# Norms at four seams of a two-layer diffusion trunk, split into token halves and placed beside weight products

## What is computed

```python
def rms_norm(x, g):
    y = xf * lax.rsqrt(jnp.mean(xf * xf, axis=-1, keepdims=True) + EPS)
    return (y * g.astype(jnp.float32)).astype(x.dtype)
def modulate(x, shift, scale):
    return x * (1 + scale) + shift
def ffn_sublayer(t, shift, scale, gate, g_pre, g_post, w_in, w_out):
    y = swiglu(modulate(rms_norm(t, g_pre), shift, scale), w_in, w_out)
    return t + FFN_RES * gate * rms_norm(y, g_post)
...
for l in range(DEPTH):
    x = ffn_sublayer(x, ...)            # sub 0, both streams
    px = project(modulate(rms_norm(x, g[2]), mx[3], mx[4]), mix_w_in[l])
    ya, yb, yc = mix_latent(...)        # three attentions
    y = merge_branches(ya, yb, yc, ...)
    x = x + mx[5] * rms_norm(y, g[3])   # sub 1
    x = ffn_sublayer(x, ...)            # sub 2
```

## Time and profile before

| | |
|---|---|
| median of 3 runs | 2990.26 us (2989.13 to 2990.41) |
| the profiled execution | 2989.05 us, its span 2987.3 us |
| PE busy | 2807.8 us, 94% |
| DVE busy | 1611.3 us, 54% |
| ACT busy | 1195.4 us, 40% |
| POOL busy | 230.9 us, 8% |
| DMA | 343.70 MB, mean 115 GB/s |

### The profile page before, as it was taken

The page is one execution under the profiler, slowest core; times in us unless marked ns, Lnnn a source line. Parts: engine busy times, 40 slices in busy tenths (PEclk is TensorE's granted clock), DMA queues, the critical chain, the costliest instruction groups (busy, mean ns, idle before and its releaser), DMA issues.

```text
span 2987.3 us, 40226 instructions
## 1 busy us (share of the span) xinstructions
PE 2807.8 (94%) x14410; PEld 2239.9 (75%) x14410; DVE 1611.3 (54%) x2722; ACT 1195.4 (40%) x2175; POOL 230.9 (8%) x321
## 2 busy tenths in 40 slices
PE   6999988999889999997999979999889989999998
PEld 4888866886656676785888848888679766869897
DVE  4677336636645444345576246773365465545764
ACT  3222324226545435434222242222343455555543
POOL 0001001101200000010000000000011020001000
PEclk8999998999999999998999989999989999999999
DMA  5455324321111122132454325553233211324554
GB/s 228 169 197 194 93 79 152 109 98 36 43 36 36 50 74 71 43 120 93 145 176 165 90 72 174 195 195 93 79 106 127 78 57 64 113 82 156 204 174 136
DMA packets 94956, 343.70 MB, mean 115 GB/s; under 512 B 10993, under 2 KB 12785, under 8 KB 92657
## 3 DMA queue, kind: packets, MB, share of 16 engines
q1 hardware_dynamic: 74850, 263.45, 26.2%
q0 software_dynamic: 19984, 78.65, 7.4%
HBM read 337.85 MB, written 4.20 MB: 115 GB/s over the span
## 4 chain that ended last, share of the span: by engine, by line
PE 78%; issue 9%; DVE 5%; ACT 5%; POOL 1%; DMA 1%; SPq 0%; POOLq 0%; DVEq 0%; ACTq 0%
PE ps L1726 20%; PE ps L1718 20%; PE ps L1719 20%; PE ps L823 3%; PE ps L785 3%; PE ps L802 2%; PE ps L1796 2%; PE ps L1778 1%; PE ps L1775 1%; PE ps L1780 1%; ACT work L1220 1%; PE ps L775 1%; DVE mx L673 1%; POOL acc L933 1%; ACT prob L589 1%
## 5 line engine op out<-in xcount | busy, mean ns | idle before, releaser
L1328 DVE TENSOR_TENSOR wlo<-raw,whi 128x1024 fp32r<-128x1024 f32 x492 | 597.8, 1224 | 689.0 <-ACT whi L1070 688.8
L1718 PE MATMUL ps<-xhi,whi 128*128 128x512 f32 (+1 forms) x2304 | 823.2, 368 | 53.2 <-DVE xlo L1562 44.8
L1719 PE MATMUL ps<-xlo,whi 128*128 128x512 f32 (+1 forms) x2304 | 811.3, 363 | 0.0
L1070 ACT ACTIVATE whi<-raw 128x1024 fp32r<-128x1024 f32 x492 | 520.6, 1058 | 564.4 <-PE ps L1726 493.9
L1718 PEld LDWEIGHTS ps<-xhi,whi 128*128 128x128 f32 x2304 | 443.8, 193 | 143.5 <-issue 44.4
L1726 PE MATMUL ps<-xhi,wlo 128*128 128x512 f32 (+1 forms) x2304 | 507.1, 363 | 0.0
L1719 PEld LDWEIGHTS ps<-xlo,whi 128*128 128x128 f32 x2304 | 445.4, 193 | 61.6
L1726 PEld LDWEIGHTS ps<-xhi,wlo 128*128 128x128 f32 x2304 | 396.1, 192 | 63.8 <-issue 0.7
L1476 DVE SCALAR_TENSOR_TENSOR work<-ada,work 128x1024 f32<-128x1024 f32 x256 | 299.5, 1221 | 0.2 <-DMA ada<-in_ada_rows 0.2
L1718 PE MATMUL ps<-ghi,whi 128*128 128x512 f32 (+1 forms) x704 | 252.2, 368 | 1.9 <-ACT whi L1070 1.9
L1719 PE MATMUL ps<-glo,whi 128*128 128x512 f32 (+1 forms) x704 | 251.8, 366 | 0.0
(11 more groups left out here) (201 smaller groups left out, 3329.1 us busy)
## 6 DMA issues: line engine op xcount, KB each, us to landing
raw<-in_ffn_in SPq DMA_DIRECT2D x176, 512.0 KB, 4.7
ada<-in_ada_rows POOLq DMA_DIRECT2D x128, 512.0 KB, 3.8
raw<-in_merge SPq DMA_DIRECT2D x96, 512.0 KB, 3.5
raw<-in_ffn_out SPq DMA_DIRECT2D x64, 512.0 KB, 3.5
raw<-in_qk_a SPq DMA_DIRECT2D x32, 512.0 KB, 3.5
raw<-in_ffn_out SPq DMA_DIRECT2D x32, 384.0 KB, 3.1
raw<-in_qk_b SPq DMA_DIRECT2D x20, 512.0 KB, 3.5
raw<-in_v_a SPq DMA_DIRECT2D x16, 512.0 KB, 3.5
```

Source lines behind the costliest of these rows:

```text
L1070: act.activation(whi[:, g.ring(SPLIT), :], raw[:, g.ring(RAW), :], ACT.Copy).then_inc(hi_ready, 1)
L1328: dve.tensor_tensor(wlo[:, g.ring(SPLIT), :], raw[:, g.ring(RAW), :], whi[:, g.ring(SPLIT), :].bitcast(F32), ALU.subtract).then_inc(lo_rea ...
L1718: pe.matmul(o, w, hi[:, first + c, 0:tk], start=start, stop=False)
L1719: pe.matmul(o, w, lo[:, first + c, 0:tk], start=False, stop=False)
```

## The change

1. The norms of the four 512-token seams are worked as two halves of 256 tokens (`half_norm`). The last products before the seam are run twice: the last 4 output tiles of `ffn_out` (12 groups), or all 8 groups of `wo`, first for tokens 0 to 255, then, with the weights loaded and split again, for tokens 256 to 511. The norm of the first half is interleaved with the second of these runs, one slot of the norm to a group (`beside`).
2. The norm of the second half is interleaved with the first products after the seam, done for the first half alone: in front of a feed-forward the first 8 groups of `ffn_in` (`head`, in eight PSUM banks), which are then run again for the second half; in front of the mixer the 10 groups of `v_b` and `v_a`, run for the first half and then for the second. The values thus come first in the mixer, ahead of the rope products. The remaining `ffn_in` has 9 bodies in place of 11 where a head was taken off (sub 2 of layer 0, sub 0 of layer 1).
3. POOL sums the squares of `x` over chunks (7 adds), and PE does one sum with ones in place of eight.
4. In all norms DVE now multiplies `x` by the scale and the inverse root in one instruction, and the shift goes in with ACT's rounding to `xhi` and with DVE's subtraction to `xlo`: ACT has one pass for a chunk in place of two. At 512 tokens each is two instructions of 256.

```diff
-TOKEN_BANKS = {"v_b": [4, 5, 6, 7], "v_a": [2, 3, 4, 5, 6, 7, 4, 5], "uv": [2, 3, 4, 5, 6, 7, 4, 5]}
+TOKEN_BANKS = {("v_b", 0): [2, 3], ("v_a", 0): [4, 5, 2, 3], ("v_b", 1): [4, 5], ("v_a", 1): [2, 3, 4, 5],
+               ("uv", 0): [2, 3, 4, 5, 6, 7, 4, 5]}
 STAT, ADA_BANK = 6, 7
+HALF_STAT = 7
+HEAD = 8
...
+def beside(norm, products):
+    for _ in products:
+        next(norm, None)
+    for _ in norm:
+        pass
...
+    def half_norm(layer, post, pre, half):
+        adds = {"stat": 2, "inv": 2, "gated": KC, "x": KC, "xsq": KC, "xsum": KC - 1, "scaled": KC, "xhi": KC,
+                "xlo": KC}
+        return add("norm", layer, post=post, pre=pre, tokens=S, span=(half * S, half * S + S), adds=adds, half=True)
+    def last_products(layer, post, pre, **kw):
+        add("y", layer, span=(0, S), fresh=not kw.get("first", 0), **kw)
+        first_half = half_norm(layer, post, pre, 0)
+        first_half.products = (add("y", layer, span=(S, T), **kw),)
...
-        def ffn(sub, tokens):
+        def ffn(sub, tokens, post, pre, head=None):
             made = vectors[(layer, sub)]
-            add("ffn_in", layer, sub=sub, tokens=tokens, iters=FC // 2, groups=4, tiles=4, vectors=made,
-                adds={"ghi": FC, "glo": FC, "made": sum(m % 3 > 0 for _, m in made)})
-            add("y", layer, src="ffn_out", sub=sub, tokens=tokens, iters=KC // 4, groups=12, tiles=4,
-                per_tile=3, adds={"sq": KC, "acc": KC})
-        ffn(0, T)
-        norm(layer, (layer, 0), (layer, 1), T)
+            first = 0
+            if head:
+                products = add("head", layer, src="ffn_in", sub=sub, tokens=S, iters=1, groups=HEAD, tiles=HEAD,
+                               head=True)
+                half_norm(layer, *head, 1).products = (products,)
+                add("ffn_in", layer, sub=sub, tokens=T, span=(S, T), iters=HEAD // 4, groups=4, tiles=4, head=True,
+                    adds={"ghi": HEAD // 2, "glo": HEAD // 2})
+                first = HEAD
+            add("ffn_in", layer, sub=sub, tokens=tokens, first=first, iters=(2 * FC - first) // 4, groups=4, tiles=4,
+                vectors=made,
+                adds={"ghi": FC - first // 2, "glo": FC - first // 2, "made": sum(m % 3 > 0 for _, m in made)})
+            kw = dict(src="ffn_out", sub=sub, tokens=tokens, groups=12, tiles=4, per_tile=3)
+            if tokens == S:
+                add("y", layer, iters=KC // 4, adds={"sq": KC, "acc": KC}, fresh=True, **kw)
+                norm(layer, post, pre, tokens)
+                return
+            kw.update(iters=1, adds={"sq": KC // 2, "acc": KC // 2})
+            add("y", layer, fresh=True, **kw)
+            last_products(layer, post, pre, first=KC // 2, **kw)
+        ffn(0, T, (layer, 0), (layer, 1), ((layer - 1, 2), (layer, 0)) if layer else None)
...
+        for half in range(2):
+            products = (
+                add("v", layer, src="v_b", cols=256, x="x", kpg=4, iters=1, groups=2, first=half, adds={"vk": 2}),
+                add("v", layer, src="v_a", cols=512, x="x", kpg=2, iters=2, groups=4, first=half, adds={"vk": 4}))
+            if half == 0:
+                half_norm(layer, (layer, 0), (layer, 1), 1).products = products
         blocks = list(range(KC)) if layer == 0 else []
+        add("rope", layer, src="qk_b", dst="q_b", first=0, tokens=nq, iters=2, groups=4, tiles=4, scale=HEAD_SCALE,
+            side=blocks[:KC // 2], adds={"rope": 8})
+        add("rope", layer, src="qk_b", dst="k_b", first=8, tokens=T, iters=1, groups=2, tiles=2, adds={"rope": 2})
...
-        add("y", layer, src="wo", sub=1, tokens=nq, iters=2, groups=4, tiles=4, per_tile=1,
-            adds={"sq": KC, "acc": KC})
-        norm(layer, (layer, 1), (layer, 2), nq)
-        ffn(2, nq)
-        norm(layer, (layer, 2), None if last else (layer + 1, 0), nq)
+        kw = dict(src="wo", sub=1, tokens=nq, iters=2, groups=4, tiles=4, adds={"sq": KC, "acc": KC})
+        if last:
+            add("y", layer, fresh=True, **kw)
+            norm(layer, (layer, 1), (layer, 2), nq)
+            ffn(2, nq, (layer, 2), None)
+        else:
+            last_products(layer, (layer, 1), (layer, 2), **kw)
+            ffn(2, nq, (layer, 2), (layer + 1, 0), ((layer, 1), (layer, 2)))
...
+            def normed_high(ph, c):
+                l, sub = ph.pre
+                act.wait_ge(done["scaled"], base(ph, "scaled") + c + 1)
+                for s in streams(ph.span):
+                    last = act.activation(xhi[:, c, sl(s)], work[:, c, sl(s)], ACT.Identity,
+                                          bias=mods[:, l, 3 * sub, c, s:s + 1])
+                last.then_inc(done["xhi"], 1)
+            def act_norm(ph):
+                inverse(HALF_STAT, ph.span, D, base(ph, "stat") + 1)
+                yield
+                yield
+                for chunks in ((0, 1, 2), (3, 4, 5), (6, 7)):
+                    for c in chunks:
+                        square(ph, c)
+                    yield
+                inverse(HALF_STAT, ph.span, D, base(ph, "stat") + 2)
+                yield
+                for chunks in ((0, 1), (2, 3, 4), (5, 6, 7)):
+                    for c in chunks:
+                        normed_high(ph, c)
+                    yield
...
+            def scaled(ph, c):
+                l, sub = ph.pre
+                for s in streams(ph.span):
+                    last = dve.scalar_tensor_tensor(work[:, c, sl(s)], x[:, c, sl(s)],
+                                                    mods[:, l, 3 * sub + 1, c, s:s + 1], inv[:, sl(s)],
+                                                    ALU.mult, ALU.mult)
+                last.then_inc(done["scaled"], 1)
+            def normed_low(ph, c):
+                l, sub = ph.pre
+                dve.wait_ge(done["xhi"], base(ph, "xhi") + c + 1)
+                for s in streams(ph.span):
+                    last = dve.scalar_tensor_tensor(xlo[:, c, sl(s)], work[:, c, sl(s)],
+                                                    mods[:, l, 3 * sub, c, s:s + 1],
+                                                    xhi[:, c, sl(s)].bitcast(F32), ALU.add, ALU.subtract)
+                last.then_inc(done["xlo"], 1)
...
+            def dve_norm(ph):
+                newton(step, dve, base(ph, "inv") + 1, HALF_STAT, ph.span, D)
+                residual_ready(ph)
+                yield
+                for chunks in ((0, 1, 2), (3, 4, 5), (6, 7)):
+                    for c in chunks:
+                        gated(ph, c)
+                    for c in chunks:
+                        added(ph, c)
+                    yield
+                yield
+                newton(step, dve, base(ph, "inv") + 2, HALF_STAT, ph.span, D)
+                yield
+                for chunks in ((0, 1), (2, 3, 4), (5, 6, 7)):
+                    for c in chunks:
+                        scaled(ph, c)
+                    for c in chunks:
+                        normed_low(ph, c)
+                    if chunks[0] != 2:
+                        yield
...
+            def pe_norm(ph):
+                def total(number):
+                    return pe.matmul(ps[:, HALF_STAT, ph.span], ones[:, :], acc[:, ph.span], start=True, stop=True)\
+                             .then_inc(done["stat"], 1)
+                pe.wait_ge(done["acc"], base(ph, "acc"))
+                pe.wait_ge(done["refined"], base(ph, "inv"))
+                wait(pe, done["yraw"], base(ph, "yraw"))
+                wait(pe, bank_free[HALF_STAT], ph.heads)
+                total(0)
+                for slot in range(10):
+                    yield
+                pe.wait_ge(done["xsum"], base(ph, "xsum") + KC - 1)
+                pe.wait_ge(done["refined"], base(ph, "inv") + 1)
+                total(1)
+                for slot in range(3):
+                    yield
+                pe.wait_ge(done["refined"], base(ph, "inv") + 2)
+                yield
```

More of the change, by code:

```diff
@@ L994, in _ @@
             for ph in plan:
[L995 removed]
+                if ph.kind == "ffn_in" and ph.vectors:
                     feed_modulation_vectors(ph)
[L997 to L1004 removed]
```

385 lines of the change are left out of this document (235 added, 150 removed).

## The result

| | before | after |
|---|---|---|
| median | 2990.34 us (2989.13 to 2991.43) | 2962.80 us (2955.31 to 2965.93) |
| ratio, 95% interval | | 0.9905 [0.9893, 0.9918] |
| the profiled execution | 2989.05 us | 2961.36 us |

The change is worth 27.5 us. The forecast was 80, and the time lies 8 us above the range's upper end. The sign was right and two thirds of the gain are missing. Where they are is plain from the profile of the changed kernel.

A forecast was written before the change was run, and what follows sets the result against it. PE, busy for 94% of the span, was taken as the bound. -142.3 + 12.7 + 5.6 + 32 + 15 - 3 = -80 us from the profiled 2989.05 gave 2909, so a median of 2910 us; range 2885 to 2955.

The forecast's parts named there:

- The seams: Four 512-token seams between sub-layers: their windows beyond useful products cost 142.3 us, all that the split can win.
- Products run twice: `ffn_out`, `wo` and `head` run as two 256-token halves cost slightly more than one 512-token run: +12.7 us.
- (c): Rival: second halves' norms stay visible, each costing 22.1 us in place of 4, four times: 2982 us; chance 0.07.
- (d): Rival: the change doesn't do what it says, all eight halves stand open, +145: 3055 us; chance 0.03.
- (e): Rival: 160 half groups go at DVE's 3.7 us in place of 2.88: 3017 us; chance 0.03.
- What of a half norm stays visible: Eight half norms: PE waits some 3 us each near DVE's last slot, plus 1 for POOL's adds: +32 us.
- its sums: PE's two sums with ones in each half norm, 16 in all, at full clock: +5.6 us.
- The 1 us for POOL's adds: Each half norm: 1 us for POOL's adds excluding DVE, most falling where DVE has slack; 8 us in all.
- Rival (b): POOL and DVE's port exclusion is paid in full, 53 us in place of 8: 2955 us; chance 0.12.
- The blocks: Layer 1's first `ffn_in`: bodies with six blocks make `wlo` late by 2.5 us in six halves: +15 us.
- Rival (a): The blocks in layer 1's first `ffn_in` cost nothing, because the third lands earlier: 2895 us; chance 0.12.
- The fold: Scale and shift folded in the 256-token seam and the first norm: -3 us together, bounds -6 and +3.

The follow-up runs named there:

- experiment 6: DVE's last slot of twelve split in two: changed kernel 2960.94 us, experiment 5's version 2916.44 us; in that version PE's second sum two places later instead: 2924.72 us.
- experiment 1: Changed kernel with vector (1, 7) made beside layer 1's last `qk_a` products, not in its first `ffn_in`, so four blocks to a body: 2937.53 us.
- experiment 5: Changed kernel with vector (1, 7) moved likewise and squares of `x` added by DVE, not POOL: 2915.39 us; with own-completion waits on DVE added: 2931.45 us.
- experiment 1's counterpart: Kernel before, with the 40 blocks of layer 1's first `ffn_in` laid on its eleven bodies, three of them with six: 3014.27 us, ratio 1.0082.
- experiment 3: Changed kernel with squares of `x` in eight buffers in place of two, still added by POOL: 2972.04 us.

## Why the prediction was wrong, point by point

- **The seams, 142.3 us.** Right, as far as a view shows it: no window of 35 us between sub-layers is left, and the halves account for the rest. The 256-token seam stayed (23.85 us in place of 24.99).
- **Products run twice, +12.7.** Right. The first run and the second half of the values keep the pace it was worked out from, with 175 and 277 GB/s of weights. Rivals (c), (d) and (e) fall: no half group outside a norm is over 2.88 us, and a second half costs 8.3 in front of the mixer and 10.3 and 14.1 in front of a feed-forward (`head` and its second half together), where (c) had 22.1.
- **What of a half norm stays visible, +32, with its sums +5.6.** This is the step that failed: 76.8 us in place of 37.6. The sums were sized right: the next product starts 0.35 us after one (419.14, 419.49), 5.6 for sixteen. The 3 us in DVE's last slot are there by size and place (3.2), but the wait on `wlo` that the prediction reasoned from is 0.96 of them, and splitting the slot gained nothing (experiment 6), so that the size fits is in part luck. The 1 us for POOL's adds was some 5.4 in the window read above. The argument was that most adds fall in slots in which DVE has slack. The slack is DVE's; the add does not wait for slack but for a gap, and until then it holds a `tmp` buffer, with ACT, the rounding of weights and PE behind it. I priced the exclusion from DVE's side only, as delay of DVE, and didn't ask who stands behind POOL. The bound of 8 x 9 us was the right size, and I had argued it away. Of the 39.2 us between 37.6 and 76.8, taking POOL out of the sums gives back 24.0 (78.6 to 54.6, experiments 1 and 5), though four adds on DVE stand in its place.
- **Rival (b), 2955.** Nearest of all (2962.80), and in its mechanism half right: the exclusion is paid, but mostly by POOL and those behind it, not by DVE. Even with POOL out of the sums the halves are 54.6 over and not 37.6. That these 17 us are DVE's, which the ledger of the prediction had just below the bound, fits the price of the gaps (experiment 5) and is not shown wait by wait.
- **The blocks, +15.** Right in mechanism, place and each of its times, mis-sized at 25 us (both ways): the waits were counted and the clock behind them was not. In the window the six waits of PE are 15.2 us together, so the 15 was right for what it counted. Of the 10 us more, 8.5 are the five stretches of 3.4 us at half the clock, 1.7 each; here nothing gives them back, since PE sets the pace in `ffn_in`. The bound of 24 was just passed, for another reason than the one given for it. Rival (a) falls.
- **The fold, -3.** Alone and in whole norms it is -6.5, of which the part that remains beside the split is the 256-token seam (0.7 alone, 1.1 in the changed kernel) and the start. The first product starts at 57.9 us after and 60.9 before, but at 59.6 in experiment 1's counterpart, where nothing changed that far, so of this 3.0 no part is shown to be the fold's.
- **Values first, 0.** No cost was seen; it was not tried by itself.

The Trainium skill ("SBUF — State Buffer", section "Who interferes with whom") says that the one who comes second at the shared port pair blocks for the whole instruction. By that rule an add that comes during `wlo` would wait 1.2 us at most. The add at 412.41 and 36 others like it in the changed kernel's trace agree. The 9 that waited for a whole train of instructions do not, and the 3.54 and 7.16 us decide. The same section's remark that order of issue decides who blocks is borne out: when POOL's add had been let in first, DVE's `work` chunks took 1.84 us for two at 413.24, where three took 1.09.

## What to carry to other kernels

When work is moved to sit beside other work, list for each helper engine not only how long its instruction takes but who stands behind it in order: a 0.7 us add that may have to wait for a gap in another engine's stream must not be followed, through a ring of two buffers, by anything the main engine needs. If the engine that paces the stretch has no slack, give it the fewest instructions and neither gaps nor partners at its port, and count the lower clock behind a wait of PE where PE sets the pace, as in `ffn_in` here; beside a late norm it was given back. Before trusting a planner's side effect (six blocks where four fitted), price it alone: here it was nearly as large as the whole gain, and was had back by moving eight blocks.

## What the runs showed of the hardware that I had not expected

- A GpSimd add of 0.72 us, begun within a train of VectorE instructions with two SBUF inputs, ended in 9 of 16 cases of the changed kernel only 0.58 to 0.6 us after the train's end: 3.54 us at 407.07, and 7.16 us in experiment 3. Where the VectorE instruction that it met had itself begun after a gap or had been held up, it ended as long after that one instruction, in all 37 cases. A gap of 0.03 us is enough: with one after each instruction the adds took 1.79 and 0.90 us.
- An own-completion wait costs VectorE 0.125 us each, and 128 of them cost the kernel 16.1 us.
- Behind five of the six waits of TensorE in the main `ffn_in` (2.1 to 3.2 us), and behind the one of 2.26 us at the first seam of experiment 5, the granted clock was at its lower level (1.2 in place of 2.4 GHz) for 3.4 us. Behind the sixth (2.00 us), behind the 2.05 us at 412.12 in the changed kernel, and behind the same 2.26 us at 1701.86 in experiment 5 it stayed at the upper one. What decides between the two was not settled here.
